# Moving three token sums and the down projections' stationary pairs to other SBUF addresses in a two-layer decoder trunk

## What is computed

```python
for i in range(2):
    z = rmsnorm(h, norm_mix_pre[i])
    z = mlstm_mixer(z, ...) if i == 0 else swa_sink_mixer(z, ...)
    h = h + rmsnorm(z, norm_mix_post[i])
    z = conv_ffn(rmsnorm(h, norm_ffn_pre[i]), f_w_up[i], f_conv_w[i], f_conv_b[i], f_w_down[i])
    h = h + rmsnorm(z, norm_ffn_post[i])

def conv_ffn(h, w_up, conv_w, conv_b, w_down):
    gate, val = jnp.split(h @ w_up, 2, axis=-1)           # 2 x 2816 features
    gp = jnp.pad(gate, ((0, 0), (CONV_W - 1, 0), (0, 0)))
    gate_c = conv_b + sum(conv_w[j] * gp[:, j:j + S] for j in range(CONV_W))
    return (jax.nn.silu(gate_c) * val) @ w_down
```

## Time and profile before

| | us |
|---|---|
| median of 3 runs (lowest to highest) | 1061.99 (1061.45 to 1062.16) |
| the profiled execution, its own time | 1061.99 |
| its span, first to last instruction | 1060.2 |
| PE busy | 1051.5 (99% of the span) |
| DVE busy | 730.1 (69%) |
| ACT busy | 531.5 (50%) |
| POOL busy | 271.9 (26%) |

### The profile page before, as it was taken

How to read it: one execution, slowest core, us unless ns; L and a number is a source line. 1 busy time by engine, 2 the same in 40 slices (tenths; PEclk the granted TensorE clock), 3 DMA queues, 4 the chain that set the end, 5 groups by cost and what they waited for, 6 DMA issues and landing times.

```text
span 1060.2 us, 18750 instructions
## 1 busy us (share of the span) xinstructions
PE 1051.5 (99%) x6822; PEld 943.5 (89%) x6822; DVE 730.1 (69%) x1013; ACT 531.5 (50%) x971; POOL 271.9 (26%) x195
## 2 busy tenths in 40 slices
PE   9999999999999999999999999999999999999997
PEld 8888888898999999988889987789999999988886
DVE  7534579588988988633366577678898898943354
ACT  6511447445565565422355367754566566542242
POOL 1000211004565565100000023300656556400000
PEclk9999999999999999999999999999999999999999
DMA  9342328233343343122272552123234334222232
GB/s 287 108 120 80 100 81 253 48 97 91 89 119 109 88 119 113 55 92 97 99 198 61 133 127 80 21 60 100 64 96 119 100 98 119 79 80 99 99 139 80
DMA packets 154828, 111.18 MB, mean 105 GB/s; under 512 B 35536, under 2 KB 140144, under 8 KB 154784
## 3 DMA queue, kind: packets, MB, share of 16 engines
q1 hardware_dynamic: 153776, 107.41, 34.5%
q0 software_dynamic: 864, 2.92, 0.9%
q10 hardware_dynamic: 144, 0.26, 0.1%
HBM read 106.87 MB, written 2.13 MB: 103 GB/s over the span
## 4 chain that ended last, share of the span: by engine, by line
PE 93%; DVE 4%; SPq 1%; ACT 1%; issue 1%; DMA 0%; DVEq 0%; ACTq 0%
PE ps L2061 11%; PE ps L2063 11%; PE ps L2062 11%; PE ps L2095 8%; PE ps L2096 8%; PE ps L2094 8%; PE ps L1808 6%; PE ps L1810 5%; PE ps L1809 5%; PE ps L2000 2%; PE ps L2002 2%; PE ps L2001 2%; PE ps L1889 1%; PE ps L1890 1%; PE ps L1891 1%; PE ps L2191 1%
## 5 line engine op out<-in xcount | busy, mean ns | idle before, releaser
L1808 PE MATMUL ps<-act_hi,w_hi 128*128 128x256 f32 (+1 forms) x440 | 144.8, 329 | 1.5 <-DVE act_lo L1153 1.4
L1809 PE MATMUL ps<-act_lo,w_hi 128*128 128x256 f32 (+1 forms) x440 | 142.4, 324 | 0.0
L1810 PE MATMUL ps<-act_hi,w_lo 128*128 128x256 f32 (+1 forms) x440 | 142.4, 324 | 0.0
L2061 PE MATMUL ps<-act_hi,w_hi 128*128 128x256 f32 x432 | 122.4, 283 | 0.0
L2062 PE MATMUL ps<-act_lo,w_hi 128*128 128x256 f32 x432 | 122.4, 283 | 0.0
L2063 PE MATMUL ps<-act_hi,w_lo 128*128 128x256 f32 x432 | 122.4, 283 | 0.0
L1604 DVE TENSOR_TENSOR w_lo<-raw,w_hi 128x1024 fp32r<-128x1024 f32 x32 | 39.2, 1225 | 117.0 <-ACT w_hi L952 117.0
L611 POOL TENSOR_TENSOR sums<-raw 128x512 f32<-128x512 f32 x36 | 48.3, 1341 | 262.3 <-PE ps L1810 139.6
L2095 PE MATMUL ps<-w_lo,w_hi 128*128 128x512 f32 x288 | 112.1, 389 | 0.0
L2094 PE MATMUL ps<-w_hi 128*128 128x512 f32 x288 | 112.1, 389 | 0.0
L2096 PE MATMUL ps<-w_hi,w_lo 128*128 128x512 f32 x288 | 112.1, 389 | 0.0
(11 more groups left out here) (267 smaller groups left out, 2839.6 us busy)
## 6 DMA issues: line engine op xcount, KB each, us to landing
raw<-in_f_w_up SPq DMA_DIRECT2D x88, 512.0 KB, 4.6
raw<-in_f_w_down SPq DMA_DIRECT2D x44, 512.0 KB, 3.2
raw<-in_m_w_in SPq DMA_DIRECT2D x23, 512.0 KB, 4.2
raw<-in_m_w_out SPq DMA_DIRECT2D x8, 512.0 KB, 3.3
raw<-in_a_w_in SPq DMA_DIRECT2D x16, 256.0 KB, 4.5
raw<-in_a_w_out SPq DMA_DIRECT2D x16, 256.0 KB, 4.7
h<-in_x SPq DMA_DIRECT2D x4, 512.0 KB, 7.9
h<-in_x_turned SPq DMA_DIRECT2D x3, 512.0 KB, 6.7
```

Of the source, the lines that this page charges most:

```text
L1808: nc.tensor.matmul(dst, uh[:, k], zh, start=(k == 0), stop=False)
L1809: nc.tensor.matmul(dst, uh[:, k], zl, start=False, stop=False)
L1810: ins = nc.tensor.matmul(dst, ul[:, k], zh, start=False, stop=(k == KT - 1))
L2061: nc.tensor.matmul(dst, uh, zh, start=(start and k == 0), stop=False, skip_group_check=not start)
```

## The change

Three kinds of addresses move; no instruction, loop or operand size changes.

- The token sums t1, t2 and t4 (high form, low form and the sum itself) begin 4, 32 and 2 float32 elements later: 16, 128 and 8 bytes. t3 stays. The buffer `t_last` grows by 32 elements, which moves the small buffers behind it by 128 bytes.
- The stationary pairs begin later in slot 2: in layer 0 by 16 bytes (j = 0) and 128 bytes (j = 1), in layer 1 by 8 bytes (j = 0) and 512 bytes (j = 1). The pair j = 1 now runs into the first elements of slot 3.
- So `freed` makes the units of slot 3 after the first down projection wait as those of slot 2 do.

```diff
     def freed(g):
         users = [q for q in range(g) if SLOT[q] == SLOT[g]]
-        if SLOT[g] == 2 and g > G_DOWN[0]:
+        if SLOT[g] in (2, 3) and g > G_DOWN[0]:
 
             users.append(G_DOWN[0] + FT - TAIL - 1)
...
-        t_last = sb("t_last", [P, 2, D], F32R)
-        t_last_sum = nc.alloc_sbuf_tensor_at("t_last_sum", [P, D], F32, offset=t_last_at + 4 * D)
-        t_early = nc.alloc_sbuf_tensor_at("t_early", [P, 4, D], F32R, offset=arena_at + 4 * 48 * KB)
+        t_last = sb("t_last", [P, 2 * D + 32], F32R)
+        t_last_sum = nc.alloc_sbuf_tensor_at("t_last_sum", [P, D + 32], F32, offset=t_last_at + 4 * D)
+        t_early = nc.alloc_sbuf_tensor_at("t_early", [P, 4 * D + 40], F32R, offset=arena_at + 4 * 48 * KB)
+        T_OFF = (4, 32, 0, 2)
...
-        t_forms = [[by_k(a[:, q + half]) for a, q in ((t_early, 0), (t_early, 2), (t_third, 0), (t_last, 0))]
+        t_third_flat = t_third[:].rearrange("p a c -> p (a c)")
+        t_forms = [[by_k(a[:, (q + half) * D + o:(q + half + 1) * D + o])
+                    for a, q, o in zip((t_early, t_early, t_third_flat, t_last), (0, 2, 0, 0), T_OFF)]
                    for half in range(2)]
         t_hi_form, t_lo_form = t_forms
-        t_sums = [by_k(a) for a in (arena[:, 52 * KB:56 * KB], arena[:, 60 * KB:64 * KB], g_pre[:], t_last_sum[:])]
+        t_sums = [by_k(a[:, q + o:q + D + o]) for a, q, o in
+                  zip((arena, arena, g_pre, t_last_sum), (52 * KB, 60 * KB, 0, 0), T_OFF)]
...
-        hid_pair = [[w[:, 2, j * HALF:(j + 1) * HALF] for w in (w_hi, w_lo)] for j in range(2)]
+        H_OFF = ((4, 32), (2, 128))
+        hid_pairs = [[[w[:].rearrange("p s c -> p (s c)")[:, 2 * D + j * HALF + o:2 * D + (j + 1) * HALF + o]
+                       for w in (w_hi, w_lo)] for j, o in enumerate(offs)] for offs in H_OFF]
```

More of the change, by code:

```diff
@@ L480, in ffn_loads @@
                 up, down = G_UP[l], G_DOWN[l]
+                hid_pair = hid_pairs[l]
                 w_up = f_w_up[l].rearrange("(k p) n -> p k n", p=P)
```

## The result

| | before | after |
|---|---|---|
| median of 4 runs each, us | 1061.81 | 1067.16 (1066.75 to 1068.19) |
| profiled execution's span, us | 1060.2 | 1064.9 |
| PE busy, us | 1051.5 | 1056.0 |

The changed kernel is **slower**: the ratio is 1.0052 with a 95% interval of 1.0035 to 1.0069, or 5.35 us. Forecast were 1059.1 us, with 1065.0 as the end of the range.

A forecast was written before the change was run, and what follows sets the result against it. PE was taken as the bound, through the distance between matmul starts. Terms -2.9 + 0 + 0 + 0 against 1061.99 us gave 1059.1 us; the range was 1053.5 to 1065.0, the forecast's own 1058 to 1060.

The forecast's parts named there:

- What bounds the kernel: Whole kernel: PE, busy 1051.5 of 1060.2 us; time is the sum of distances between matmul starts.
- The stationary pairs: Down projections, 864 matmuls of 512 columns: weight load hides in 227 ns, so 0 for all four distances.
- rival 3: Down projections: pairs gain as well, by a constant excess per matmul; times 1057.7 to 1051.9 us; chance 0.12.
- t4's 8 bytes: Up projection, t4 at 200 in the place of 192 bytes: stays nearest to its own row, 0.
- rival 4: Up projection: t4 loses its fast pace at 200 bytes, no multiple of 64; +2.9 us, time 1064.9; chance 0.16.
- The 1.7 us allowed for a start that is no multiple of 16 bytes: Up projection, t4: bound on the slowdown from its odd start, 4 ns on each of 432 matmuls.
- t2 at 128 bytes: Up projection: t2 turns fast, 2.2 us, and t4 behind it gains 0.7; together 2.9 us faster.
- t1 at 16 bytes: Up projection: at most 2.9 us gain, taken as 0 because 16 bytes is nearest to no distance.
- rival 2: Up projection: any distance that breaks the step helps, so t1 and t2 both gain; -5.8 us, time 1056.2; chance 0.15.
- Writers, the wait, the small buffers: ACT and DVE writes stay hidden, the wait added by `freed` is already met, moved small buffers cost nothing: 0.
- Whether the others could keep up: Up projection's loop: DVE has 0.35 us per block free, so a block shorter by 0.08 us passes through.
- rival 1: All matmuls: nothing moves, as 128, 16 and 8 bytes may flip nothing; time 1062.0 us; chance 0.24.

The follow-up runs named there:

- t4_only_8: Kernel before with one shift alone, t4 8 bytes further (200 in the place of 192 off the weights' step): ratio 1.0032, 3.4 us slower.
- sums4_192: Kernel before with all four token sums, t3 too, 192 bytes off the weights' step: 1056.49 us, ratio 0.9953.
- tokens_192: Kernel before with the token operands and all buffers behind them 192 bytes off the weights' step, t4 kept at 192: 1058.84 us, ratio 0.9965.
- t4_in_step: Kernel before with 320 bytes of padding ahead of t4's buffer, so t4 lies in step with the weights: ratio 1.0025, 2.7 us slower.
- all_96: Kernel before with 96 bytes of padding ahead of the weight buffers, so all operands move together and distances stay: 1062.34 us in one run.

## Why the prediction was wrong, point by point

- **What bounds the kernel: right.** PE's starts are all that moved; waits and the other engines stayed.
- **The stationary pairs, taken as 0: the largest failure**, 3.5 of the 5.35 us. The step read the 188 ns of t4's weight loads against the 192 of t2's as the weight load being what a bad address slows, and concluded that a load has 227 ns to hide in. In the changed kernel line 2104 shows the opposite (durations ns min/median/max, first and last start):

```profile
L2104 PEld LDWEIGHTS ps<-w_hi x288: 187/188/192, 440.9 to 1036.8; 128*128 128x128 f32 x144
L2104 PE MATMUL ps<-w_hi x288: 387/392/405, 441.0 to 1037.0; 128*128 128x512 f32 x144
```

  The load's median stays at 188 and the matmul's goes from 389 to 392, while the starts move apart by up to 6.4 ns: a load at its fast value doesn't say that the address is good. The bounds for this term were also drawn on one side only. A gain of 4.3 us was allowed for, but the cost was argued away with the transposes of the earlier trace rows, which have 128 moving columns and another type, while a nearer row, of the same type and the same stationary shape with 256 moving columns, had the 6 to 7 ns that an address is worth in the earlier trace rows. That, times 864, would have put the bound of the loss at +5.8 us. It measured +6.4 ns at 16 bytes. The reading by which a pair could gain (rival 3) has no run for it: no distance is under 226.7 ns.
- **t4's 8 bytes, taken as 0: wrong.** It was put as rival 4 with 0.16. The rival's price was right: 2.2 us for t4, 36 x (1.447 - 1.379) = 2.4 us measured, and 2.9 for t4 and its tail, 3.1 in t4_only_8. Its reason, that 200 is no multiple of 64, isn't what the runs show: 256 and 320 fail as well. The 1.7 us allowed for a start that is no multiple of 16 bytes was too much: at 184 and 200 bytes t4 is 0.005 to 0.007 us over the 1.440 of a product in step, some 0.2 us in 36 blocks.
- **t2 at 128 bytes, taken as -2.9 us: wrong.** It measured 1.438 us, next to nothing. "Far from both 0 and 512" was no measure of a good distance.
- **t1 at 16 bytes, taken as 0: too low by 0.5 us**, and rival 2 was right about the sign: 1.407 in the place of 1.421.
- **Writers, the wait, the small buffers, taken as 0: right.** Whether the others could keep up wasn't put to the test here, as the blocks grew longer. But the part that gives out first is not the one named (DVE's line 1520): in sums4_192, at 9.76 us per block, and in tokens_192 it is ACT's copy of z1a's result.
- **The page's rule** (rival 1). The Trainium skill (SBUF — State Buffer, "SBUF: two separate sides") says that "PE, ACT, and DVE's dedicated pair never wait on anyone". The prediction took this further, to say that no start address matters to a matmul; the page has nothing on two operands of PE itself. The runs don't agree with that reading: t4_in_step and t4_only_8 cost 2.7 and 3.4 us by one operand's address alone, and all_96 keeps every pace when both move.

So the sign was wrong for two reasons that added up: a mechanism for the sums that was seen in one row and carried to distances it doesn't hold for (t2's 128 and t4's 200 bytes), and a mechanism for the pairs (a slow load, hidden behind 512 columns) under which no address could cost anything, where they cost 3.5 us.

## What to carry to other kernels

Where TensorE is the bound and a line's matmuls come at two paces for one shape, look at the distance between moving and stationary operand in SBUF, by starts in the timeline and not by durations. A distance that works in one shape is a measured point: here 192 bytes were worth 5.6% of a 256-column matmul (113.3 ns against 120.0), 8 bytes to either side lost it, and with 512 columns no distance tried beat a multiple of 512 bytes. So copy the very distance that a fast row shows, for that shape alone. Price leaving it as the loss of the whole gain, and don't take a wide matmul for safe because its weight load has room: here leaving the step cost up to 7.4 ns of 226.7. Then look for the engine that PE will wait for at the new pace; here it was ACT, whose copy ended 0.32 to 0.61 us ahead of its use in the kernel before (its first block aside) and late in the faster ones.

## What the runs showed that was not expected

- Paces carry over: t1 at distance 0 takes 1.421 us behind a fast t4 and 1.440 behind a slow one, and one distance, 192 bytes, ran at 1.360 us per product and, behind a wait for ACT, at 1.412.
- The loss isn't a matter of alignment alone: for the pairs 8 bytes cost 4.0 ns per matmul, 96 bytes 7.4, 256 bytes 1.1.
- What happens inside the chip, and why 192 is a good distance for 256 columns and not for 512, no run here shows.
